# Four weight tensors laid out by the host in the order of use, and no TensorE transposes of U and of the keys

## What is computed

```python
qy = (xb @ w_query).reshape(PEER_BLOCK, PEER_HEADS, 2, PEER_DQ // 2)
s = jnp.einsum('phcd,hckd->phck', qy, sub_keys)       # 8 heads x 2 halves, 128 keys
top_s, top_i = lax.top_k(s, PEER_TOPK)                # 16 of 128, twice
...                                                   # 16 best of the 16 x 16 sums: experts, gate
u = expert_u[experts]                                 # expert_u, expert_v: (16384, 1024)
act = jax.nn.gelu(jnp.einsum('pd,phkd->phk', xb, u), approximate=False)
return jnp.einsum('phk,phkd->pd', gate * act, expert_v[experts])
```

## Time and profile before

| | us |
|---|---|
| median of 3 runs | 5222.47 |
| lowest and highest | 5221.14 and 5224.43 |
| the profiled execution, its own time | 5226.25 |
| its span, first to last instruction | 5224.4 |
| TensorE matmuls busy | 4495.2 (86%) |
| VectorE busy | 2505.9 (48%) |
| ScalarE busy | 1256.4 (24%) |
| mean granted TensorE clock | 0.906 |

### The profile page before, as it was taken

How to read it: one execution, slowest core, us unless ns; L and a number is a source line. 1 busy time by engine, 2 the same in 40 slices (tenths; PEclk the granted TensorE clock), 3 DMA queues, 4 the chain that set the end, 5 groups by cost and what they waited for, 6 DMA issues and landing times. The chain is left out here.

```text
span 5224.4 us, 67609 instructions
## 1 busy us (share of the span) xinstructions
PE 4495.2 (86%) x22202; PEld 3782.7 (72%) x22202; DVE 2505.9 (48%) x5840; ACT 1256.4 (24%) x1733; POOL 170.6 (3%) x259
## 2 busy tenths in 40 slices
PE   6699755557768799888888799999899999999997
PEld 1699745556556677677777688888678888888886
DVE  0322265544356677666667511111155555555554
ACT  0200143332121122244444311111121111111110
POOL 0000011101000000000000000000000000000000
PEclk9799865568878899999999899999999999999998
DMA  5222100012211122145455522222244333343332
GB/s 210 98 94 89 63 23 22 22 46 92 86 41 34 43 78 80 69 110 132 125 132 143 125 93 88 90 91 88 101 173 144 145 144 145 145 145 145 145 145 99
DMA packets 444640, 533.20 MB, mean 102 GB/s; under 512 B 280210, under 2 KB 315234, under 8 KB 443490
## 3 DMA queue, kind: packets, MB, share of 16 engines
q1 hardware_dynamic: 411556, 419.71, 24.4%
q0 software_dynamic: 26624, 99.63, 5.8%
q10 hardware_dynamic: 6336, 12.58, 0.6%
HBM read 369.30 MB, written 162.55 MB: 102 GB/s over the span
## 5 line engine op out<-in xcount | busy, mean ns | idle before, releaser
L322 PE MATMUL evo<-vhi,Hhi 128*128 128x512 f32 x2048 | 797.6, 389 | 30.6 <-DVE Hlo L1571 30.6
L323 PE MATMUL evo<-vlo,Hhi 128*128 128x512 f32 x2048 | 797.4, 389 | 0.0
L324 PE MATMUL evo<-vhi,Hlo 128*128 128x512 f32 x2048 | 797.2, 389 | 0.0
L1584 DVE TENSOR_TENSOR acc<-acc,evo 128x512 f32<-128x512 f32 x512 | 352.1, 688 | 620.1 <-PE evo L324 620.1
L322 PEld LDWEIGHTS evo<-vhi,Hhi 128*128 128x128 f32 x2048 | 385.0, 188 | 110.9 <-issue 31.0
L323 PEld LDWEIGHTS evo<-vlo,Hhi 128*128 128x128 f32 x2048 | 384.9, 188 | 79.8
L324 PEld LDWEIGHTS evo<-vhi,Hlo 128*128 128x128 f32 x2048 | 384.9, 188 | 79.8
L1135 DVE TENSOR_TENSOR aulor<-atbr,auhir 128x512 fp32r<-128x512 f32 x128 | 88.5, 692 | 684.0 <-ACT auhir L1130 670.4
L322 PE MATMUL apar<-h2hi,auhir 128*128 128x512 f32 x1024 | 405.3, 396 | 0.0
L324 PE MATMUL apar<-h2hi,aulor 128*128 128x512 f32 x1024 | 400.1, 391 | 0.0
L323 PE MATMUL apar<-h2lo,auhir 128*128 128x512 f32 x1024 | 399.2, 390 | 0.0
(11 more groups left out here) (275 smaller groups left out, 7678.2 us busy)
## 6 DMA issues: line engine op xcount, KB each, us to landing
gates_dram<-gstage SPq DMA_DIRECT2D x16, 4096.0 KB, 21.5
vraw<-in_expert_v SPq DMA_DIRECT2D x128, 512.0 KB, 3.3
ga<-ahead_dram SPq DMA_DIRECT2D x128, 512.0 KB, 4.2
gr<-gates_dram SPq DMA_DIRECT2D x128, 512.0 KB, 5.5
aurr<-in_expert_u POOLq DMA_DIRECT2D x64, 512.0 KB, 3.5
ahead_dram<-ager SPq DMA_DIRECT2D x128, 256.0 KB, 2.0
gwi<-in_w_in POOLq DMA_DIRECT2D x16, 1216.0 KB, 6.7
proj_dram<-gyi SPq DMA_DIRECT2D x128, 152.0 KB, 1.8
```

The source lines that it names most:

```text
L322: pe.matmul(out, lhi, rhi, start=(k == 0), stop=False)
L323: pe.matmul(out, lhi, rlo, start=False, stop=False)
L324: return pe.matmul(out, llo, rhi, start=False, stop=(k == n - 1))
L1584: dve.tensor_tensor(at, at, vo[u % BANKS][:, :], ALU.add).then_inc(vo_add.sem, 1)
```

## The change

The host writes four inputs in another order before the launch. For U, row i becomes [1024 as 8 x 128 on partitions][128 experts], that is, already transposed: a partition's piece is again 4096 bytes in one run. The keys are stored transposed, in runs of 512 bytes as before. w_query and w_in are stored by block, so that a partition's piece of a block is one run (4096 and 9728 bytes). On the chip `Ahead.transpose` and its calls go, with the PSUM banks `atb`; both cuts of a row become one instruction each, of 1024 columns, and read the loaded row in SBUF; ScalarE waits for the load itself. The refill of a buffer waits for the low cut of the row two before, as it did. In route the transpose of the keys and their copy go, and TensorE waits for the loaded keys ahead of the score matmuls. Counts of semaphore slots change to keep the orders that the transposes had kept.

```diff
-                        sp.dma_start(w[:, p], wv[:, :, bass.ds(c * P, P)]).then_inc(w_in[p], 16)
-                        sp.wait_ge(k_mm.sem, k_mm.free(c))
-                        sp.dma_start(kraw[:, p], kv[bass.ds(c, 1)].rearrange("o k d -> (o k) d")).then_inc(k_in[p], 16)
+                        sp.dma_start(w[:, p], w_query[bass.ds(c, 1)].rearrange("o p k n -> (o p) k n")).then_inc(w_in[p], 16)
+                        sp.wait_ge(s_mm.sem, s_mm.free(c * 2 + 1))
+                        sp.dma_start(kT[:, p], sub_keys[bass.ds(c, 1)].rearrange("o d k -> (o d) k")).then_inc(k_in[p], 16)
...
-                        act.wait_ge(k_cp.sem, k_cp.free(c))
+                        act.wait_ge(q_mm.sem, q_mm.free(c * 2 + 1))
                         act.activation(whi[:, p], w[:, p], ACT.Copy).then_inc(hi_done.sem, 1)
-                        act.wait_ge(k_mm.sem, k_mm.done(c))
-                        act.activation(kT[:, p], pk[:, :], ACT.Copy).then_inc(k_cp.sem, 1)
...
-                        pe.transpose(pk[:, :], kraw[:, p], K.ident[:, :]).then_inc(k_mm.sem, 1)
...
     def load(self, eng, r, p, row):
 
-        eng.wait_ge(self.ut_rows.sem, self.ut_rows.free(r))
-        eng.dma_start(self.ur[:, p], self.u[bass.ds(row * P, P), :]).then_inc(self.u_in[p].sem, 16)
+        eng.wait_ge(self.ulo_done.sem, self.ulo_done.free(r))
+        eng.dma_start(self.ur[:, p], self.u[bass.ds(row, 1)].rearrange("o p k e -> (o p) k e")).then_inc(self.u_in[p].sem, 16)
...
-    def transpose(self, pe, r, p, at):
-        pe.wait_ge(self.u_in[p].sem, self.u_in[p].value(at))
-        for c in range(2):
-
-            pe.wait_ge(self.ulo_done.sem, self.ulo_done.free(r * 2 + c))
-            for k in range(4):
-                last = pe.transpose(self.tb[c][:, k * P:(k + 1) * P], self.ur[:, p, (4 * c + k) * P:(4 * c + k + 1) * P], self.K.ident[:, :])
-            last.then_inc(self.ut_mm.sem, 1)
...
-    def cut_high(self, act, r, p):
-        for c in range(2):
-            act.wait_ge(self.ut_mm.sem, self.ut_mm.done(r * 2 + c))
-            act.activation(self.uhi[:, p, 4 * c:4 * c + 4], self.tb[c][:, :].rearrange("p (k e) -> p k e", k=4), ACT.Copy).then_inc(self.uhi_done.sem, 1)
+    def cut_high(self, act, r, p, at):
+
+        act.wait_ge(self.u_in[p].sem, self.u_in[p].value(at))
+        act.wait_ge(self.a_mm.sem, self.a_mm.free(r * 2 + 1))
+        act.activation(self.uhi[:, p], self.ur[:, p], ACT.Copy).then_inc(self.uhi_done.sem, 1)
...
+        link.eng.wait_ge(self.uhi_done.sem, self.uhi_done.done(r))
+        link(link.eng.tensor_tensor(self.ulo[:, p], self.ur[:, p], self.uhi[:, p].bitcast(F32), ALU.subtract), self.ulo_done.sem)
...
+    if name == "expert_u":
+        return a.reshape(NKEYS, NKEYS, KD, P).transpose(0, 3, 2, 1)
+    if name == "sub_keys":
+        return a.reshape(HC, NKEYS, P).transpose(0, 2, 1)
+    if name == "w_query":
+        return a.reshape(KD, P, HC, P).transpose(2, 1, 0, 3)
+    if name == "w_in":
+        return a.reshape(KD, P, IN_BLOCKS, D_IN // IN_BLOCKS).transpose(2, 1, 0, 3)
```

More of the change, by code:

```diff
@@ L349, in _ @@
                         pool.wait_ge(lo_done.sem, lo_done.free(b + s))
[L350 removed]
+                        pool.dma_start(w[:, s], wsrc[bass.ds(b + s, 1)].rearrange("o p k n -> (o p) k n")).then_inc(w_in[s].sem, 16)
             @block.scalar
@@ L983, in _ @@
             def _(sp):
-                for steps in (hi_done, lo_done, q_mm, q_cp, k_mm, k_cp, s_mm, s_cp, top_done):
+                for steps in (hi_done, lo_done, q_mm, q_cp, s_mm, s_cp, top_done):
                     steps.open(sp)
@@ L1067, in _ @@
                             pe.wait_ge(q_cp.sem, q_cp.done(c * 2 + h))
-                            pe.wait_ge(k_cp.sem, k_cp.done(c))
+                            if h == 0:
+                                pe.wait_ge(k_in[p], turn * 16 + 16)
                             pe.wait_ge(s_cp.sem, s_cp.free(c * 2 + h))
@@ L1202, in tile @@
                         if not (last and j == R - 1):
-                            A.cut_high(act, r + 1, 1 - j % 2)
+                            A.cut_high(act, r + 1, 1 - j % 2, (t * (R // 2) + (j + 1) // 2) * 16 + 16)
                         for h in range(2):
@@ L1207, in tile @@
                     act.activation(best[:, :, :], best[:, :, :], ACT.Exp).then_inc(be_done, 1)
-                A.cut_high(act, 0, 0)
+                A.cut_high(act, 0, 0, 16)
                 turns(act, tile)
@@ L1275, in tile @@
                         r, p = t * R + j, j % 2
-                        if not (last and j == R - 1):
-                            A.transpose(pe, r + 1, 1 - p, (t * (R // 2) + (j + 1) // 2) * 16 + 16)
                         for h in range(2):
@@ L1284, in tile @@
                     step.then_inc(pick_mm, 1)
-                A.transpose(pe, 0, 0, 16)
                 turns(pe, tile)
@@ L1352, in _ @@
                 with dve.Fori(0, NB // 2 - 1) as turn:
-                    link.enter(turn, 2 * 2 * ROWS_BLOCK)
+                    link.enter(turn, 2 * ROWS_BLOCK)
                     body(turn, False)
@@ L1373, in body @@
                             A.multiply(pe, b * 2 + j, j, h, range(c, c + CH))
-                            if k == 3 and not (last and half == 1 and j == ROWS_BLOCK - 1):
-                                A.transpose(pe, b * 2 + (j + 1), 1 - j, (b + j) * 16 + 16)
-                A.transpose(pe, 0, 0, 16)
                 turns(pe, body)
@@ L1394, in body @@
                                 if not (last and half == 1 and j == ROWS_BLOCK - 1):
-                                    A.cut_high(act, b * 2 + (j + 1), 1 - j)
+                                    A.cut_high(act, b * 2 + (j + 1), 1 - j, (b + j) * 16 + 16)
                             if k == 0 and gi:
@@ L1455, in body @@
                         if not (last and p):
-                            A.cut_high(act, r + 1, 1 - p)
+                            A.cut_high(act, r + 1, 1 - p, (turn + p) * 16 + 16)
                         for h in range(2):
                             A.gelu(act, r, h)
-                A.cut_high(act, 0, 0)
+                A.cut_high(act, 0, 0, 16)
                 turns(act, body)
@@ L1473, in _ @@
                 with dve.Fori(0, ROWS // 2 - 1) as turn:
-                    link.enter(turn, 4)
+                    link.enter(turn, 2)
                     body(turn, False)
@@ L1483, in body @@
                         r = turn * 2 + p
-                        if not (last and p):
-                            A.transpose(pe, r + 1, 1 - p, (turn + p) * 16 + 16)
                         for h in range(2):
                             A.multiply(pe, r, p, h, range(KD))
-                A.transpose(pe, 0, 0, 16)
                 turns(pe, body)
```

48 lines of the change are left out of this document (19 added, 29 removed).

## The result

The kernel before took 5223.45 us (median of 4, 5221.14 to 5231.32) and the changed one 5086.11 us (median of 4, 5084.1 to 5089.7), a ratio of 0.9736 with a 95% interval of 0.9722 to 0.9751. It is faster, as forecast, but by 137 us where 110 were forecast: 5086 lies 26 us under the forecast of 5112, and 8 us under the low end of the range. The profiled execution took 5085.53 us, with a span of 5083.7 and a mean granted clock of 0.908.

A forecast was written before the change was run, and what follows sets the result against it. TensorE's queue was taken to bound rest, with engine handovers taking part of best, gate and route. Gains of 56.6 + 26.6 + 23.6 + 2.2 + 1.0 = 110 us from the median 5222.47 gave 5112 us, range 5094 to 5140.

The forecast's parts named there:

- Part 1: Rest: 62 rows inside TensorE's stream each lose 0.913 us of transposes, the new cuts stay hidden; 56.6 us gained.
- Part 2: Best: 23 rows within tiles gain 0.913 us each, seven tile starts 0.8 us each; 26.6 us gained.
- Part 3: Gate: 31 rows lose 0.87 us of transposes, less 0.11 for a longer chain through the cuts; 23.6 us gained.
- Part 4: Starts of rest, best and gate: first matmuls come 1.72, 1.72 and 1.0 us earlier, halved for low clock; 2.2 us gained.
- half is kept: Starts of three stages: if the clock rises at the same moment as before, 2.2 us of 4.4 remain.
- the rule of the Trainium skill: Transposes don't count as busy TensorE as matmuls do; removal would cost the clock nothing, total 2.2 us more.
- Part 5: Route and loads: keys' transpose lies in a hole, 0 us; w_query and w_in landings 0.5 us each; 1.0 us gained.
- The clock misses the transposes: At 26 places in route, tile ends and starts, one more low clock stretch each costs 27 us: 5139; chance 0.12.
- Gate is set by its chain: The handover between VectorE and TensorE, not TensorE's queue, sets gate's first groups; gate gives nothing: 5136; chance 0.09.
- More gain than summed: Whole kernel: gain beyond the sum of the parts, down to 5090 us; chance 0.05.
- No gain: U's transposes only nominally in the way, time returns in a DMA, store or barrier: within 0.2%, 5222; chance 0.03.
- slower: ScalarE sits behind U's landing; at 25 us a landing, 2.0 us more in 96 rows: 5414; chance 0.01.

The follow-up runs named there:

- e10: Changed kernel with eight unused transposes of a constant ahead of each of 63 rows' matmuls in rest: 5150.49 us, 0.9863 against the kernel before.
- e11: Changed kernel with one unused matmul of 512 columns added to each row of best: 5094.19 us, 0.976 against the kernel before.
- e12: Changed kernel with two unused matmuls of 512 columns in one row of each tile of best: 5094.19 us, 0.9753 against the kernel before.
- e1: Changed kernel with four unused matmuls of 512 columns behind group 3 of each row in gate: 5134.68 us, 0.983 against the kernel before.
- e3: Changed kernel with two unused matmuls of 512 columns behind group 3 of each row in gate: 5117.84 us, 0.979 against the kernel before.
- second pair of traces: Both kernels run again with nothing changed: 5222.51 us before, 5091.26 us after, 0.9744 against the kernel before.
- e9: Kernel before with only the new layouts of w_in, w_query and keys and the changed route code; U still transposed on chip: 5221.08 us, 0.9993.
- e5: Changed kernel with gate's high cut moved up to group 2 and low cut to group 4: 4977.74 us, 0.9532 against the kernel before.
- e8: Changed kernel with gate's cuts, best's Exp and route's high cut all moved earlier: 4859.31 us, 0.9302 against the kernel before.

## Why the prediction was right and where it failed

**Part 1, rest, held.** 55.8 us for 56.6; rows of 10.88 as computed; the cuts hidden; e10 gives the price back by itself, 55.4. The first row of the stage shows the 2.5 us from cut to matmul.

**Part 2, best, had the work right and the clock wrong.** The three inner rows of a tile are 10.88 us each and its end 1.06 us shorter, as worked out (1.07). The step that failed is the one that took each tile's clock as unchanged, but for half of the 1.07: the low time rose from 32 to 51 us, which cost 7 us, and the idle time by 2.4 us. Measured 18.4 for 26.6. e11 and e12 show the same from the other side. VectorE's wait before `rden` fell from 8.5 to 7.0 us a tile and not to 5: the tile lost 2.4 us and not 3.5, and VectorE itself has 0.7 us less to do in it (316.12 us before, 310.78 after, over 8 tiles).

**Part 3, gate, is the term that made the error.** Forecast 23.6, measured 51.9. Two steps of it failed: the charge for a longer chain, and the clock taken as unchanged. The smaller one: 0.11 us a row were charged for a longer chain and weren't paid. The low cut ends 4.79 us after group 4 starts, before 4.72, but the one-hot row behind it follows after 0.34 instead of 0.42 us, so that a row at full clock gained 0.90 and not 0.76 (4 us in all). The larger: the part counted work at full clock only. The bounds, 12.4 to 27.0, allowed for a second low stretch as a loss, and none for fewer of them. The low time fell from 103 to 46 us, worth 26, and e1 to e3 bring it back with the length of the row. The earlier trace rows had the hint, a clock of 0.92 in a stage with a hole in every row; the prediction looked at the clock at starts and tile ends, and not at what follows a hole of gate.

**Part 4, starts.** The first matmul of rest came 1.70 us earlier against the first step on U, as computed (1.72), and another 0.7 between gate's last matmul and U's landing. The three gaps between the stages gave 6.1 us, where the sum had 4.4 before it took off half for the clock. What the clock took is in the stages behind the gaps, and it scatters more than this. After the change it is still at the low level when as long has passed after the first matmul of best and of rest as it took to rise in the earlier trace rows:

```profile
1774.00:1776.00 2.00, 2.00 (x6) 1.52 (x6) 1.85 (x3) 1.65 (x2) 0.00 (x0) 0.50 0.69 260
...
2932.00:2933.00 1.00, 1.00 (x4) 0.81 (x3) 0.00 (x0) 0.00 (x0) 0.00 (x0) 0.50 0.90 340
```

By the clock records it rose 3.4 us after the first matmul of best and 5.6 after that of rest, so 2.1 and 1.3 us later than before, or 1.7 us of lost time. But in the second pair of traces it rose earlier after the change than before, in best after 3.1 us for 3.6 and in rest after 3.3 for 4.4, and in e9, whose rows of U are those of before, after 4.4 and 1.7. So the step "half is kept" is neither shown nor refuted. Nor do these runs decide on the rule of the Trainium skill at the starts, and the 1.3 us of best, which the prediction held against it, was the draw of one trace: the same code has 3.6 and 4.4 us in two others. The part's lower end was summed wrongly too: at half speed a rise 1.72 us later costs 0.86 us, so it is -0.4 and not -0.7.

**Part 5.** Route is the same within 0.3 us at the same 70 us low: the keys' transpose lay in the hole. The landings gained 0.3 and 0.9 us. The stretch between the input projection and route, in which no line was changed, is 6.5 us shorter in this pair of traces. Over all runs the kernels built on before had 854.4 to 857.6 us there and those built on after 849.6 to 855.1. The means, of 3 and of 12 traces, are 856.0 and 852.2 us, so some 4 us of the 6.5 may belong to the change and the rest is scatter; what would make them stays open.

**The sum.** 140.7 measured less 110 is 30.7: gate +28.3, best -8.2, starts +3.9, the unchanged stretches, route and the loads +7.5, rest -0.8. The prediction's ends of 89 and 127 us are not what its parts' bounds add up to, which is 93 and 122.5; the measured time lies beyond either.

**The rivals.** "The clock misses the transposes" was the right subject with the wrong place and sign for the largest part: in route, where it was priced, nothing was lost, and at the starts nothing that stands out of the scatter; it came true in best alone, for 7 us. "Gate is set by its chain", which had gate give nothing, is refuted by the 51.9 us and by e1 to e3, where TensorE's queue alone got longer and the stage by more than that; the hole in each row is set by the chain even so, as e5 shows. "No gain" and "slower" are out: in rest TensorE is busy for 698.80 of 698.80 us, and behind the first two rows of a stage no cut waits for U's landing. "More gain than summed" was what happened, and 5090 was too near an end for it, since no bound of the parts stood for a clock that gains.

## What to carry to other kernels

Work that lies in the queue of an engine that never waits is worth its start-to-start price, read where that row stands next to one without it, and moving it to the host gives that back in full. In a stage with holes in every row or tile that price isn't enough: read the clock of the stage, take up to half of its low time as what can be won with the same holes (gate won 26 of 51 us), allow for a loss beside it (best lost 7), and put both signs into the range. Once a dependency is gone, look at what still stands where the dependency had put it: in gate moving both cuts up gave 108 us. And look at the order of the other in-order queues as well: with the Exp and route's cut moved up too it was 227 us, more than the 137 of the change itself.

## What the runs showed of the hardware

Holes of equal length, 2.37 us, were followed by the low level of the clock or not: 87 to 94 us of idle time in gate went with 103, 91, 64 or 46 us of low clock, more for the longer rows, whatever filled them. With nothing changed in gate it was 33 to 49 us from trace to trace. In best 3.6 or 7.3 us of added work left the tile at 51 us and the stage 1.4 or 1.6 us longer. With the holes closed (e5 to e8) the stages have a granted clock of 0.99 to 1.00.

A high and a low cut of 1024 columns from SBUF take 2.30 us from the start of the one to the end of the other (2407.65 to 2408.72 + 1.23), hardly more than the 2.22 us of the two pairs of 512 columns from PSUM that they replace. And the place of one Exp decided here whether the stage behind it loads ScalarE's tables 14 times at 1.28 us, or not at all.
